# Head pairs side by side in the two halves of the array: two attentions in a two-block kernel

## The chip, the cores and the metric

The kernel runs on one core of a Trainium2 chip, as one program. The metric is the device time of one launch in microseconds; three runs of the kernel before gave 2449.45 to 2453.14, median 2451.6. Engines are named as in the profile: PE is TensorE's matmul, PEld its weight load, DVE is VectorE, ACT is ScalarE, POOL is GpSimd, SP issues the transfers. All engines work through their own instructions in order and meet at semaphores.

## The reference

Two transformer blocks over 512 tokens of width 1024, all in fp32. The first block mixes tokens in two ways side by side and then applies a product-key expert layer (PEER). The second block has two causal attentions side by side. What the change touches is this:

```python
# first block, neighbourhood attention: 8 heads of 64; a query sees a window of 8 x 32 grid keys (masked to 16)
# with a bias, and 256 context keys, in one softmax
s_win = einsum('bcqhd,bkcjhd->bhcqkj', q_r, kb) * scale
s_win = where(col_ok, s_win + bias, -inf)
s_ctx = einsum('bcqhd,blhd->bhcql', q_r, k_ctx) * scale
p = softmax(concatenate([s_win, s_ctx], -1))
o = einsum(p_win, vb) + einsum(p_ctx, v_ctx)
# beside it: a bidirectional gated linear recurrence, 4 heads of 128 (S_t = diag(f_t) S_{t-1} + k_t v_t)

# second block, stick-breaking attention, 8 heads of 64, causal, blocks of 128 queries
z = einsum('bhqd,bhkd->bhqk', qb, k) * scale
suffix = reverse_cumsum(log_sigmoid(-z)) - log_sigmoid(-z)
w = where(strict, exp(log_sigmoid(z) + suffix), 0);  out = w @ v
# second block, latent attention, 8 heads, query and key of 64 + 32, value of 64
sc = (q_nope . k_nope + q_pe . k_pe) * scale
p = softmax(where(causal, sc, -inf));  out = p @ v
```

## The kernel before

Tokens are columns and features are partitions; a matmul takes its stationary operand as 128 partitions by up to 128 columns. fp32 matmuls appear in the trace as two records each, transposes as one. PSUM has 8 banks of 128 x 512.

**Mixing stage** (`phase_mix`, lines 571 to 1012). `items` are 32: head pair hp, query block c of 128, and head s of the pair, in that order, so that items 2m and 2m+1 are the two heads of one pair for one query block. Work goes in 36 slots; slot n holds one item at several stages and, from `fill[n]`, one or two steps of the recurrence (44 steps in four units, of which each has the levels 0 to 9 and a read-out; two context steps ahead, two norms behind). The order in each engine's stream is written out by hand:

- PE (lines 812 to 827): `scores(n)` (two products of 256 columns, contraction 64), the recurrence steps (a level is 8 products of 128 columns), `turn(n-2)` (four transposes), `values(n-3)` (four products whose output has 64 rows).
- DVE (lines 1000 to 1012): the recurrence step (`level`: three products in place, then `copied`, two copies out of PSUM), then `item(n)` (lines 899 to 912: add bias or zero and take the maximum), then `inverse(n-1)`.
- ACT (lines 855 to 893): exponential of n, scaling of n-1, copy of the transposed n-2 out of PSUM (`turned_sb`), and every other slot the attention output of a pair.
- POOL (line 686): one product of each level.

`s_sb`, where `item(n)` writes, has three buffers, so `item(n)` waits until `turn(n-3)` is done (line 904). The scores have two PSUM banks, the transposes and the values one each.

**Second block** (`second_block`, line 1812 on). `items` are 64: first the 32 of the stick-breaking kind, then the 32 of the latent one, in each head by head and then by query block i of 128 (the keys seen, `width`, are 128(i+1)). The slots follow the items. Between them stand the products of the weights ("tiles", `TILES2`, each out of a piece of 128 x 1024 weights that ACT rounds to a high part, line 2049, and DVE turns into a low part, line 2177): 20 tiles (`uqm`, `kn`, `kv`) in the stick half, 20 (`sz` 4, `ga` 8, `bra` 8) in the soft half. A tile is three matmuls for each of its input blocks. `AHEAD` is 3: in slot n PE does `scores(n)`, `turn(n-3)`, `values(n-4)` and then the tiles; DVE does `mask(n)`, `finish(n-1)`, low parts, a store every fourth slot and the evacuations of the slot before; ACT does `exps(n)`, high parts, the copy of the transposed n-3, evacuations. In the stick half the query of an odd head has zeros in its lower 64 rows and that of an even head in its upper 64, so that the products contract over all 128 rows; POOL writes the zeros (lines 1912 to 1916), ACT copies a query tile in two halves (lines 2069 and 2070). The value product of a head computes the 128 columns of its pair, and the store (line 2274) takes the 64 rows that are the head's.

## Time and profile before

| | us |
|---|---|
| Median of 3 runs (lowest, highest) | 2451.6 (2449.45, 2453.14) |
| Profiled execution: own time | 2451.39 |
| its span | 2449.6 |
| PE busy in the span | 2250.8 (92%) |
| DVE busy | 1780.1 (73%) |
| ACT busy | 924.3 (38%) |
| POOL busy | 629.7 (26%) |
| Mixing stage, from and to | 291.9 to 526 |
| Second block's attention, stick half, from and to | 2040 to 2151 |
| soft half, from and to | 2151 to 2294 |

A share of busy time is a mean over stages with different limits. PE is busy nearly all the time in the expert layer between 526 and about 1930 us, which the change doesn't touch. In the stages that it touches, PE and DVE work in turns, so one reads there which engine waits, for what, and what is queued behind the waiting instruction.

### The profile page before, as it was taken

How to read it: one execution, taken by the hardware profiler on the slowest of the kernel's cores; microseconds unless marked ns; L12 is line 12 of the kernel's file. 1: busy time of each engine (PE TensorE's matmuls, PEld its weight loads, DVE VectorE, ACT ScalarE, POOL GpSimd, SP SyncE). 2: the span in 40 equal slices, each digit the busy share in tenths (PEclk: the TensorE clock that was granted, in tenths of full speed). 3: DMA queues.
4: the chain of work that ended last, by engine and by line, in shares of the span. 5: the costliest groups of instructions: out<-in, count | busy, mean ns of one | idle time of the engine just before them, and what ended most of it. 6: DMA issues, size and time to landing. Idle time of an engine off the chain costs nothing. (4 is left out here: it accounts for less than half of the span.)

```text
span 2449.6 us, 32335 instructions
## 1 busy us (share of the span) xinstructions
PE 2250.8 (92%) x12803; PEld 2017.8 (82%) x12803; DVE 1780.1 (73%) x2985; ACT 924.3 (38%) x1210; POOL 629.7 (26%) x357
## 2 busy tenths in 40 slices
PE   5999887978998999999999899999999897889997
PEld 3888676756898999899999899999999676677775
DVE  7555687763689999999995687788786657754543
ACT  4222233333232333455553233333333534566332
POOL 0000232311346776533224433333331000000000
PEclk8999998989999999999999999999999999999999
DMA  6567400011236777688889999999996222111221
GB/s 250 206 239 243 146 8 1 1 69 52 94 111 224 238 243 250 248 309 342 322 332 367 361 350 354 361 348 353 359 351 215 79 78 86 44 52 61 78 86 69
DMA packets 178103, 488.73 MB, mean 200 GB/s; under 512 B 13696, under 2 KB 80384, under 8 KB 166432
## 3 DMA queue, kind: packets, MB, share of 16 engines
q1 hardware_dynamic: 141088, 352.43, 41.6%
q0 software_dynamic: 36864, 134.23, 14.2%
q8 instruction: 102, 1.67, 0.3%
q14 instruction: 49, 0.40, 0.1%
HBM read 432.08 MB, written 52.43 MB: 198 GB/s over the span
## 5 line engine op out<-in xcount | busy, mean ns | idle before, releaser
L1066 PE MATMUL ps<-h_high,u_high 128*128 128x384 f32 (+1 forms) x1216 | 430.8, 354 | 43.4 <-POOL u_low L1256 19.1
L1067 PE MATMUL ps<-h_low,u_high 128*128 128x384 f32 (+1 forms) x1216 | 421.4, 347 | 0.0
L1068 PE MATMUL ps<-h_high,u_low 128*128 128x384 f32 (+1 forms) x1216 | 421.2, 346 | 0.0
L1066 PE MATMUL ps<-w_high,v_high 128*128 128x384 f32 x1024 | 344.5, 336 | 10.0 <-DVE w_low L1636 10.0
L1067 PE MATMUL ps<-w_low,v_high 128*128 128x384 f32 x1024 | 343.5, 335 | 0.0
L1068 PE MATMUL ps<-w_high,v_low 128*128 128x384 f32 x1024 | 343.4, 335 | 0.0
L1066 PEld LDWEIGHTS ps<-h_high,u_high 128*128 128x128 f32 x1216 | 231.0, 190 | 58.7 <-POOL u_low L1256 22.1
L1393 ACT ACTIVATE v_high<-v_raw 128x2048 fp32r<-128x2048 f32 x64 | 122.6, 1916 | 346.8 <-PE ps L1068 346.8
L1066 PE MATMUL ps<-h_high,w_high 128*128 128x512 f32 x560 | 227.7, 407 | 25.6 <-DVE h_low L2289 10.3
L1067 PEld LDWEIGHTS ps<-h_low,u_high 128*128 128x128 f32 x1216 | 231.4, 190 | 8.3 <-issue 1.2
L1068 PEld LDWEIGHTS ps<-h_high,u_low 128*128 128x128 f32 x1216 | 231.0, 190 | 8.0
L1067 PE MATMUL ps<-h_low,w_high 128*128 128x512 f32 x560 | 221.8, 396 | 0.0
L1068 PE MATMUL ps<-h_high,w_low 128*128 128x512 f32 x560 | 221.2, 395 | 0.0
L1624 DVE TENSOR_TENSOR v_low<-v_raw,v_high 128x2048 fp32r<-128x2048 f32 x64 | 146.7, 2293 | 101.8 <-ACT v_high L1393 101.8
L1247 POOL DMA_INDIRECT mixT<-in_peer_v,row_index x102 | 147.5, 1446 | 252.3 <-DVE row_sum L1668 235.9
L1066 PEld LDWEIGHTS ps<-w_high,v_high 128*128 128x128 f32 x1024 | 193.4, 189 | 10.6 <-DVE v_low L1624 7.4
L1247 POOL DMA_INDIRECT mixT<-in_peer_u,row_index x103 | 137.9, 1339 | 249.4 <-DVE row_dot L1592 220.8
L1067 PEld LDWEIGHTS ps<-w_low,v_high 128*128 128x128 f32 x1024 | 193.6, 189 | 0.0
L1068 PEld LDWEIGHTS ps<-w_high,v_low 128*128 128x128 f32 x1024 | 193.4, 189 | 0.0
L1459 ACT ACTIVATE gelu<-ps 128x384 f32<-128x384 f32 x128 | 63.7, 500 | 303.4 <-PE ps L1068 161.9
L2177 DVE TENSOR_TENSOR w_low<-w_raw,w_high 128x1024 fp32r<-128x1024 f32 x69 | 84.6, 1226 | 124.7 <-ACT w_high L2049 124.6
L1066 PEld LDWEIGHTS ps<-h_high,w_high 128*128 128x128 f32 x560 | 107.1, 191 | 57.1 <-issue 14.6
(428 smaller groups left out, 4436.8 us busy)
## 6 DMA issues: line engine op xcount, KB each, us to landing
v_raw<-in_peer_v SPq DMA_DIRECT2D x64, 1024.0 KB, 6.8
w_raw<-in_w SPq DMA_DIRECT2D x99, 512.0 KB, 3.7
u_first<-in_uT SPq DMA_DIRECT2D x32, 1024.0 KB, 6.5
u_second<-in_uT SPq DMA_DIRECT2D x32, 1024.0 KB, 6.7
xT<-in_late_w SPq DMA_DIRECT2D x56, 512.0 KB, 4.4
gelu_up<-gelu SPq DMA_DIRECT2D x128, 192.0 KB, 7.2
gates<-gates_sb SPq DMA_DIRECT2D x12, 2048.0 KB, 12.9
weighted<-gelu_up SPq DMA_DIRECT2D x64, 384.0 KB, 6.9
```

The source lines that it names most:

```text
L1066: pe.matmul(out, wh, mh, start=start, stop=False)
L1067: pe.matmul(out, wh, ml, start=False, stop=False)
L1068: return pe.matmul(out, wl, mh, start=False, stop=stop)
L1247: pool.indirect_dma_start(out=row_of(total), out_offset=None, in_=table, in_offset=bass.IndirectOffsetOnAxis(ap=row_no[:, n:n + 1], axis=0))\
L1393: act.activation(v_high[:, g % 2], v_raw[:, g % 2], ACT.Copy).then_inc(v_hi, 1)
L1459: act.activation(gel[:, x % 4, :], ps[:, x % 4, 0:DENSE], ACT.Gelu).then_inc(u_ev, 1)
L1624: dve.tensor_tensor(v_low[:, g % 2], v_raw[:, g % 2], v_high[:, g % 2].bitcast(F32), ALU.subtract)\
L2177: dve.tensor_tensor(wlo[:, i % SPLITS, :], raw[:, i % RAWS, :], whi[:, i % SPLITS, :].bitcast(F32), ALU.subtract).then_inc(w_low, 1)
```

## The change

Both attentions go by head pairs.

In the mixing stage, PE computes the scores of items n and n+1 together in even slots, first the window product of one head on rows 0 to 63 and of the other on rows 64 to 127, then the same for the context keys. The value products of both heads of the pair n-4 are done in even slots too, block by block in turns, one in the left and one in the right 64 columns, and now ahead of the transposes. DVE takes the item of an odd slot ahead of its recurrence steps, that of an even slot behind them as before, and waits for the scores of the pair. The number of buffers stays.

In the second block the items of a pair stand side by side in the list, and a slot is a pair (34 slots for 69). PE: `scores(p)`, tiles, `values(p-2)`, two transposes of p-1. DVE: two masks, low parts with the evacuations of the same slot, a store, two finishes. ACT: two `exps`, high parts with evacuations, two copies. The stick-breaking scores contract over 64 rows, the heads of a pair in the two halves; the zeros, the waits for them and the second query buffers go. The value products are 64 columns wide, two side by side; a store takes a whole pair, so there are 8 instead of 16. The `ga` tiles come ahead of the `sz` tiles, and the soft half takes them from its first slot on.

The diff, with its small renamings (`AHEAD + 1` to 4, the `scored` wait of `mask` as in `item`) left out:

```diff
@@ -688,17 +688,18 @@
         def _(pe):
-            def scores(i):
-                h, c = items[i]
-                a, hp = DH * (h % 2), h // 2
+            def scores_of_pair(i):
+                hp, c = items[i][0] // 2, items[i][1]
                 if i >= 2:
-                    pe.wait_ge(maxed, 2 * (i - 1))
-                q = k.qT[a:a + DH, hp, c * P:(c + 1) * P]
+                    pe.wait_ge(maxed, 2 * i)
                 k0 = min(max(QB * c - KB // 4, 0), GW - KB)
-                win = k.kT[a:a + DH, hp, 0:T].rearrange("p (r x) -> p r x", r=ROWS)[:, :, k0:k0 + KB]
-                pe.matmul(ps[:, i % 2, 0:WIN], q, win, start=True, stop=True)
-                pe.matmul(ps[:, i % 2, WIN:512], q, k.kT[a:a + DH, hp, T:T + C], start=True, stop=True)\
-                  .then_inc(scored, 1)
+                rows = [slice(0, DH), slice(DH, P)]
+                for s, a in enumerate(rows):
+                    win = k.kT[a, hp, 0:T].rearrange("p (r x) -> p r x", r=ROWS)[:, :, k0:k0 + KB]
+                    pe.matmul(ps[:, s, 0:WIN], k.qT[a, hp, c * P:(c + 1) * P], win, start=True, stop=True)
+                for s, a in enumerate(rows):
+                    pe.matmul(ps[:, s, WIN:512], k.qT[a, hp, c * P:(c + 1) * P], k.kT[a, hp, T:T + C], start=True,
+                              stop=True).then_inc(scored, 1)
@@ -708,18 +709,19 @@
-            def values(i):
-                h, c = items[i]
-                pair = i // 2
-                pe.wait_ge(turned_sb, i + 1)
-                if i % 2 == 0 and pair:
-                    pe.wait_ge(stored, pair)
-                a = DH * (h % 2)
+            def values_of_pair(i):
+                first_head, c = items[i]
+                pe.wait_ge(turned_sb, i + 2)
+                if i:
+                    pe.wait_ge(stored, i // 2)
                 for j in range(4):
-                    v = (k.vw[:, 2 * c + j, :] if j < 2 else k.vc[:, j - 2, :])[:, h * DH:(h + 1) * DH]
-                    last = pe.matmul(ps[a:a + DH, 3, 0:P], v, pT[:, i % 2, j * P:(j + 1) * P],
-                                     start=j == 0, stop=j == 3)
-                last.then_inc(summed, 1)
+                    v = k.vw[:, 2 * c + j, :] if j < 2 else k.vc[:, j - 2, :]
+                    for s in range(2):
+                        h = first_head + s
+                        last = pe.matmul(ps[DH * s:DH * (s + 1), 3, 0:P], v[:, h * DH:(h + 1) * DH],
+                                         pT[:, s, j * P:(j + 1) * P], start=j == 0, stop=j == 3)
+                        if j == 3:
+                            last.then_inc(summed, 1)
@@ -810,8 +812,8 @@
             for n in range(SLOTS_N):
-                if n < N:
-                    scores(n)
+                if n < N and n % 2 == 0:
+                    scores_of_pair(n)
                 for kind, x, s in fill[n]:
@@ -821,10 +823,10 @@
                         norms(x)
+                if 0 <= n - 4 < N and n % 2 == 0:
+                    values_of_pair(n - 4)
                 if 0 <= n - 2 < N:
                     turn(n - 2)
-                if 0 <= n - 3 < N:
-                    values(n - 3)
...
@@ -880,7 +882,7 @@
                     if i >= 2:
-                        act.wait_ge(summed, i - 1)
+                        act.wait_ge(summed, 2 * (i // 2))
                     if i == 0:
...
@@ -899,7 +901,7 @@
                 dve.wait_ge(table, variant[c] + 1)
-                dve.wait_ge(scored, n + 1)
+                dve.wait_ge(scored, 2 * (n // 2) + 2)
                 if n >= 3:
...
@@ -998,12 +1000,14 @@
             for n in range(SLOTS_N):
+                if n < N and n % 2:
+                    item(n)
                 for kind, x, s in fill[n]:
                         read_out(x)
-                if n < N:
+                if n < N and n % 2 == 0:
                     item(n)
...
@@ -1726,10 +1730,10 @@
     piece("kv", 0, [("kv", t) for t in range(4)])
+    for i in range(8):
+        piece("ga", i, [("ga", i)])
     for i in range(4):
         piece("sz", i, [("sz", i)])
-    for i in range(8):
-        piece("ga", i, [("ga", i)])
     for i in range(4):
...
@@ -1815,8 +1818,9 @@
     TT = T // P
-    items = [(kind, h, i) for kind in ("stick", "soft") for h in range(NH) for i in range(TT)]
+    items = [(kind, 2 * hp + s, i) for kind in ("stick", "soft") for hp in range(NH // 2) for i in range(TT) for s in range(2)]
     N = len(items)
+    PAIRS, HALF = N // 2, N // 4
     TB = (6, 7)
...
@@ -1880,13 +1881,13 @@
-        early, late = list(range(PROJECTED, tile_no("sz", 0))), list(range(tile_no("sz", 0), ATTENDED))
-        slots = N + AHEAD + 2
-        fill = {n: [] for n in range(slots)}
+        early, late = list(range(PROJECTED, tile_no("ga", 0))), list(range(tile_no("ga", 0), ATTENDED))
+        slots = PAIRS + 2
+        fill = {p: [] for p in range(slots)}
         for x, j in enumerate(early):
-            fill[1 + x * 31 // len(early)].append(j)
+            fill[x * HALF // len(early)].append(j)
         for x, j in enumerate(late):
-            fill[N // 2 + 4 + x * (N // 2 - 4 + AHEAD) // len(late)].append(j)
+            fill[HALF + x * (slots - HALF) // len(late)].append(j)
...
@@ -1908,12 +1909,6 @@
             pool.memset(prod[:, T - 1:T], 1.0).then_inc(made, 1)
-            pool.wait_ge(made, 3)
-            pool.memset(sq[DH:P], 0.0).then_inc(zeroed, 1)
-            for hp, odd in enumerate(q_odd):
-                pool.wait_ge(zeroed, hp + 1)
-                pool.memset(odd[0:DH], 0.0).then_inc(zeroed, 1)
-            pool.wait_ge(zeroed, 5)
             pool.wait_ge(made, 3)
...
@@ -1975,43 +1970,46 @@
-            def scores(n):
-                kind, h, i = items[n]
-                if n >= 2:
-                    pe.wait_ge(acted, n - 1)
-                if n == 0:
+            def scores(p):
+                kind, h, i = items[2 * p]
+                if p:
+                    pe.wait_ge(acted, 2 * p)
+                if p == 0:
                     pe.wait_ge(act_read, read_by(BY_ACT, PROJECTED))
-                if n == N // 2:
-                    pe.wait_ge(act_read, read_by(BY_ACT, tile_no("sz", 0)))
-                    pe.wait_ge(dve_read, read_by(BY_DVE, tile_no("sz", 0)))
+                if p == HALF:
+                    pe.wait_ge(act_read, read_by(BY_ACT, tile_no("ga", 0)))
+                    pe.wait_ge(dve_read, read_by(BY_DVE, tile_no("ga", 0)))
                     pe.wait_ge(mk_rot, 1)
-                if n == 0:
-                    pe.wait_ge(zeroed, 5)
-                if kind == "stick":
-                    q, key = q_odd[h // 2] if h % 2 else sq[:, h // 2], sk[:, h // 2]
-                else:
-                    q, key = mq[0:QKD, h], mk[0:QKD, h]
-                pe.matmul(ps[:, n % 2, 0:width(n)], q[:, i * P:(i + 1) * P], key[:, 0:width(n)], start=True,
-                          stop=True).then_inc(scored, 1)
+                for s in range(2):
+                    if kind == "stick":
+                        a = slice(DH * s, DH * (s + 1))
+                        q, key = sq[a, h // 2], sk[a, h // 2]
+                    else:
+                        q, key = mq[0:QKD, h + s], mk[0:QKD, h + s]
+                    pe.matmul(ps[:, s, 0:width(2 * p)], q[:, i * P:(i + 1) * P], key[:, 0:width(2 * p)], start=True,
+                              stop=True).then_inc(scored, 1)
                 for j in range(items[n][2] + 1):
-                    last = pe.transpose(ps[:, 2 + n % 2, j * P:(j + 1) * P], w[:, n % (AHEAD + 1), j * P:(j + 1) * P], k.ident[:])
+                    last = pe.transpose(ps[:, 2 + n % 2, j * P:(j + 1) * P], w[:, n % 4, j * P:(j + 1) * P], k.ident[:])
                 last.then_inc(turned, 1)
-            def values(n):
-                kind, h, i = items[n]
-                v, head = (sv if kind == "stick" else mv), n // TT
-                pe.wait_ge(turned_sb, n + 1)
-                if n % TT == 0 and head >= 2:
-                    pe.wait_ge(stored, head - 1)
+            def values(p):
+                kind, h, i = items[2 * p]
+                v, heads = (sv if kind == "stick" else mv), p // TT
+                pe.wait_ge(turned_sb, 2 * p + 2)
+                if i == 0 and heads >= 2:
+                    pe.wait_ge(stored, heads - 1)
                 for j in range(i + 1):
-                    last = pe.matmul(ps[:, 4 + head % 2, i * P:(i + 1) * P], v[:, j, h // 2 * P:(h // 2 + 1) * P],
-                                     pT[:, n % 2, j * P:(j + 1) * P], start=j == 0, stop=j == i)
-                last.then_inc(summed, 1)
+                    for s in range(2):
+                        last = pe.matmul(ps[DH * s:DH * (s + 1), 4 + heads % 2, i * P:(i + 1) * P],
+                                         v[:, j, (h + s) * DH:(h + s + 1) * DH], pT[:, s, j * P:(j + 1) * P],
+                                         start=j == 0, stop=j == i)
+                        if j == i:
+                            last.then_inc(summed, 1)
@@ -2020,15 +2018,16 @@
                     last.then_inc(n_sum, 1)
-            for n in range(slots):
-                if n < N:
-                    scores(n)
-                if 0 <= n - AHEAD < N:
-                    turn(n - AHEAD)
-                if 0 <= n - AHEAD - 1 < N:
-                    values(n - AHEAD - 1)
-                for j in fill[n]:
+            for p in range(slots):
+                if p < PAIRS:
+                    scores(p)
+                for j in fill[p]:
                     tile(j)
+                if p >= 2:
+                    values(p - 2)
+                if 1 <= p <= PAIRS:
+                    turn(2 * p - 2)
+                    turn(2 * p - 1)
             for j in range(ATTENDED, len(TILES2)):
...
                 if n >= 2:
-                    act.wait_ge(summed, n - 1)
+                    act.wait_ge(summed, 2 * (n // 2))
                 act.activation(pT[:, n % 2, 0:width(n)], ps[:, 2 + n % 2, 0:width(n)], ACT.Copy).then_inc(turned_sb, 1)
...
@@ -2138,18 +2135,17 @@
                         act.activation(ghi[:, t, :], M[:, t, :], ACT.Copy).then_inc(t_high, 1)
-            for n in range(slots):
-                if n < N:
-                    exps(n)
-                for j in fill[n]:
+            for p in range(slots):
+                if p < PAIRS:
+                    exps(2 * p)
+                    exps(2 * p + 1)
+                for j in fill[p]:
                     if j in FIRST2:
                         high(TILES2[j][2] + 1)
-                if 0 <= n - AHEAD < N:
-                    turned_out(n - AHEAD)
-                for j in fill[n - 1] if n else []:
                     evac(j)
-            for j in fill[slots - 1]:
-                evac(j)
+                if 1 <= p <= PAIRS:
+                    turned_out(2 * p - 2)
+                    turned_out(2 * p - 1)
             for j in range(ATTENDED, len(TILES2)):
...
-            def store(head):
-                dve.wait_ge(summed, TT * head + TT)
-                if head == 0:
+            def store(heads):
+                dve.wait_ge(summed, 2 * TT * (heads + 1))
+                if heads == 0:
                     dve.wait_ge(mk_rot, 1)
-                rows = slice(DH * (head % 2), DH * (head % 2) + DH)
-                o = (so if head < NH else mo)[rows, head // 2 % 4, :]
-                dve.tensor_copy(o, ps[rows, 4 + head % 2, :]).then_inc(stored, 1)
+                o = (so if heads < NH // 2 else mo)[:, heads % (NH // 2), :]
+                dve.tensor_copy(o, ps[:, 4 + heads % 2, :]).then_inc(stored, 1)
@@ -2325,20 +2320,19 @@
             dve.wait_ge(made, 3)
-            for n in range(slots):
-                if n < N:
-                    mask(n)
-                if 0 <= n - 1 < N:
-                    finish(n - 1)
-                for j in fill[n]:
+            for p in range(slots):
+                if p < PAIRS:
+                    mask(2 * p)
+                    mask(2 * p + 1)
+                for j in fill[p]:
                     if j in FIRST2:
                         low(TILES2[j][2] + 1)
-                if n >= TT + AHEAD + 1 and (n - AHEAD - 1) % TT == 0:
-                    store((n - AHEAD - 1) // TT - 1)
-                for j in fill[n - 1] if n else []:
                     evac(j)
-            for j in fill[slots - 1]:
-                evac(j)
+                if p >= 2 and (p - 2) % TT == TT - 1:
+                    store((p - 2) // TT)
+                if p < PAIRS:
+                    finish(2 * p)
...
```

## Rows read from the trace of the kernel before

**Rows 1.** Busy time by stretch: start:end, length, us of each engine, PEclk.

```profile
291.90:526.00 234.10, 198.24 (x1288) 162.18 (x1288) 170.16 (x380) 84.50 (x168) 76.27 (x42) 0.96 0.04 14
...
2040.00:2151.00 111.00, 89.36 (x460) 68.81 (x461) 87.63 (x156) 59.77 (x139) 0.00 (x0) 0.96 0.16 53
2151.00:2294.00 143.00, 133.82 (x680) 108.16 (x679) 76.98 (x187) 85.12 (x146) 0.00 (x0) 1.00 0.18 60
```

**Rows 2.** Timeline of mixing, DVE: start, us, engine, line, op, count [idle before].

```profile
362.75 0.41 DVE L905 CUSTOM_DVE_ANT_1 s_sb<-ps,bias 128x256 f32<-128x256 f32 x1
...
363.69 0.67 DVE L961 TENSOR_TENSOR qd<-hq,fx 128x512 f32<-128x512 f32 x1
...
365.72 1.35 DVE L930 COPY_PREDICATED A_diag<-pred,ps 128x512 f32<-128x512 uint8 x2
...
367.06 0.42 DVE L905 CUSTOM_DVE_ANT_1 s_sb<-ps,bias 128x256 f32<-128x256 f32 x1
```

**Rows 3.** The same timeline, PE.

```profile
358.50 0.70 PE L699 MATMUL ps<-kT,qT 64*128 64x256 f32 x2
...
365.80 0.70 PE L699 MATMUL ps<-kT,qT 64*128 64x256 f32 x2
...
366.86 2.05 PE L759 MATMUL ps<-qd,kd 128*128 128x128 f32 x16
...
368.74 0.60 PE L708 MATMUL ps<-ident,s_sb 128*128 128x128 f32 x4
...
369.27 0.65 PE L720 MATMUL ps<-w_raw,vw 128*64 128x128 f32 x4
...
370.29 0.70 PE L699 MATMUL ps<-kT,qT 64*128 64x256 f32 x2
```

**Rows 4.** Waits in mixing: who <- for whom: us in total, times, longest.

```profile
DVE s_sb L905 <- PE ps L700: 34.4, 4, 11.4
```

**Rows 5.** Timeline of PE in mixing, after gaps.

```profile
297.02 2.05 PE L735 MATMUL ps<-ic,qd 128*128 128x128 f32 x16 [2.98 <-ACT qd L869]
...
459.12 3.63 PE L776 MATMUL ps<-qd,kd 128*128 128x256 f32 x8 [3.26 <-ACT w_raw L838]
...
508.79 1.97 PE L776 MATMUL ps<-qd,kd 128*128 128x256 f32 x8 [2.21 <-ACT w_raw L838]
```

**Rows 6.** Timeline of PE in mixing, a read-out with full-height products.

```profile
348.53 1.03 PE L801 MATMUL ps<-w_raw,ix 128*128 128x256 f32 x4
349.39 1.02 PE L793 MATMUL ps<-qd,ctx_state 128*128 128x512 f32 x2
```

**Rows 7.** Groups, 2040 to 2296: line, engine, op | busy us, mean ns | idle.

```profile
L2177 DVE TENSOR_TENSOR w_low<-w_raw,w_high 128x1024 fp32r<-128x1024 f32 x28 | 34.3, 1225 | 33.8 <-ACT w_high L2049 33.8
L2259 DVE TENSOR_TENSOR_SCAN at_prod<-at_rest,zeros 128x127 f32<-128x127 f32 (+3 forms) x32 | 26.1, 816 | 1.0 <-ACT at_rest L2101 0.5 <-issue 0.2
L2262 DVE TENSOR_TENSOR at_w<-at_w,at_prod 128x128 f32<-128x128 f32 (+3 forms) x32 | 15.8, 492 | 1.1
...
L2188 DVE TENSOR_TENSOR soft_out<-ps,cosT 32x512 f32<-32x512 f32 x8 | 5.5, 689 | 0.2
...
L2049 ACT ACTIVATE w_high<-w_raw 128x1024 fp32r<-128x1024 f32 x28 | 29.5, 1054 | 0.0
...
L2100 ACT ACTIVATE at_w<-ps 128x128 f32<-128x128 f32 (+3 forms) x32 | 14.1, 440 | 46.5 <-DVE ps L2245 46.5
```

**Rows 8.** Soft half: the gate chain, a tile on PE (timeline), and PE's waits.

```profile
2160.96 1.28 ACT L2087
...
2165.07 0.69 DVE g_low L2203
...
2219.35 0.48 PE L1066 MATMUL ps<-h_high,w_high 128*128 128x512 f32 x1
...
2224.89 0.59 PE L1994 MATMUL ps<-mqkv 96*128 96x256 f32 x2
...
PE ps L2012 <- ACT at_wT L2110: 8.6, 11, 1.4
```

More of the change, by code:

```diff
@@ L1747 @@
 TILES2, PIECES2, PROJECTED, ATTENDED = second_tiles()
-AHEAD = 3
 BY_ACT = {"cq", "ckv", "sq", "sk", "uqm", "kn", "kv", "sz", "ga", "mz", "gb"}
@@ L1830, in second_block @@
         ghi, glo = sb("g2_high", [P, 5, T], F32R), sb("g2_low", [P, 5, T], F32R)
-        w = sb("at_w", [P, AHEAD + 1, T])
+        w = sb("at_w", [P, 4, T])
         rest = sb("at_rest", [P, 2, T])
@@ L2094, in exps @@
                 act.wait_ge(masked, n + 1)
-                if n > AHEAD:
-                    act.wait_ge(turned, n - AHEAD)
+                if n >= 4:
+                    act.wait_ge(turned, n - 3)
                 if kind == "stick":
@@ L2241, in mask @@
                 W = width(n)
-                dve.wait_ge(scored, n + 1)
+                dve.wait_ge(scored, 2 * (n // 2) + 2)
                 diag = ps[:, n % 2, W - P:W]
@@ L2260, in finish @@
                                                 initial=1.0, op0=ALU.mult, op1=ALU.add))
-                    own = w[:, n % (AHEAD + 1), 0:W]
+                    own = w[:, n % 4, 0:W]
                     dve.tensor_tensor(own, own, prod[:, T - W:T], ALU.mult).then_inc(ready, 1)
@@ L2327, in _ @@
             dve.wait_ge(made, 3)
-            for n in range(slots):
-                if n < N:
-                    mask(n)
-                if 0 <= n - 1 < N:
-                    finish(n - 1)
-                for j in fill[n]:
+            for p in range(slots):
[3 more added lines that the diff above has]
+                for j in fill[p]:
                     if j in FIRST2:
                         low(TILES2[j][2] + 1)
-                if n >= TT + AHEAD + 1 and (n - AHEAD - 1) % TT == 0:
-                    store((n - AHEAD - 1) // TT - 1)
-                for j in fill[n - 1] if n else []:
                     evac(j)
-            for j in fill[slots - 1]:
-                evac(j)
+                if p >= 2 and (p - 2) % TT == TT - 1:
+                    store((p - 2) // TT)
+                if p < PAIRS:
+                    finish(2 * p)
+                    finish(2 * p + 1)
             for j in range(ATTENDED, len(TILES2)):
```

13 lines of the change are left out of this document (4 added, 9 removed).

## The prediction

> **What bounds the kernel now.** I read the busy shares by stretch first, since the diff touches only the mixing stage and the second block's attention. Outside them nothing changes but a few short operations. In the mixing stretch (234 us), VectorE is busy 170 us and PE 198 us; in the two halves of the second attention (111 and 143 us) PE is busy 89 and 134 us [rows 1]. Then the timelines, for how the engines interlock.
>
> In mixing, a slot is one attention item beside one or two steps ("levels") of the recurrence. VectorE: an item with its reciprocal takes 363.69 - 362.75 = 0.94 us, a level 367.06 - 363.69 = 3.37 (three products, 2.03, then two copies of 0.67, 1.34 together, that wait for the level before on PE). Nothing is idle between these [rows 2]. PE, same slot: scores 1.06, level 1.88, transposes 0.53, value product 1.02, together 4.49 us from scores to scores, without a gap [rows 3]. So a slot with one level takes 4.49 us (PE just above VectorE's 4.31), one with two 365.80 - 358.50 = 7.3 (VectorE's turn: 4.31 + 3.3). Both engines are full at once, and each level on PE needs VectorE's copies of the same level: the reader should see a loop with no slack on either side. VectorE's idle time is nearly all in four waits for scores, 34.4 us [rows 4], where a read-out ends a unit.
>
> **Mixing: the new wait.** VectorE has three buffers for the scores it reads (s_sb, item n uses n mod 3), so item n waits until item n-3 has been transposed (`turned`). PE transposes n-3 in slot n-1, after that slot's level. Before, VectorE did the level of slot n first and the item last, so the transposes had a whole level (3.37) to get done. The change puts the item of each odd slot ahead of its level. VectorE then reaches item n (odd) right after item n-1, while PE still has the level of slot n-1 to do, now two items' value products ahead of the transposes too. Behind the waiting item stand VectorE's level, its copies, PE's next level, POOL's product and ScalarE's exponential.
>
> I time it from the end of VectorE's copies in the even slot. PE's level may start 0.1 after the first of the two copies, so at -0.67 + 0.1, and ends 1.88 later, at 1.31. Then two value products V, transposes 0.53 + 0.13 to land (0.7 with the semaphore), then VectorE's item 0.87, three products 2.03, first copy 0.67, and PE's odd level 0.1 + 1.88. Then transposes 0.53, pair scores S, and PE's next even level 1.88.
>
> V and S are not in the trace. Upper ends, no two matmuls side by side: V = 2 x 1.02 = 2.04, S = 2 x 1.06 = 2.12 [rows 3]. Lower ends: a 128-column full-height fp32 record takes 1.88/16 = 0.118 us, and each fp32 product is two records on the same half of the array; the order is two records in one half, two in the other, so a record can pair only with its neighbour over the change of half: 16 value records fit in 9 times, 8 score records in 5. That gives V = 9 x 0.118 = 1.06 and S = 5 x 0.26 = 1.3. The 0.26 is a row of its own kind: 256-column records in half the rows come 1.06/4 = 0.265 us apart [rows 3], full-height ones (349.39 - 348.53)/4 = 0.215 [rows 6]; so half height alone is no gain, only company is. I take the lower ends, since the two halves read other partitions and write other banks or partitions.
>
> The Trainium skill, "TensorE: Matmul & The Clock Gate", Part 3 (Measured speedup vs the span model), gives 3.07 times for four row tiles at once, which speaks for the lower ends; "TensorEngine Tiling (Array Packing)", Key Properties, says that a change of tiling mode drains the engine, which speaks against the change in the second attention. No row here shows two tiles together. The changes of form in rows 3 cost at most some 0.05 us each.
>
> With the lower ends a pair of single-level slots takes 1.31 + 1.06 + 0.7 + 0.87 + 2.03 + 0.67 + 0.1 + 1.88 + 0.53 + 1.3 + 1.88 = 12.33, less the first 1.31, since it is counted from one end of PE's even level to the next: 11.0 us, against 2 x 4.49 = 8.98: +2.0. VectorE alone would need 1.31 + 1.06 + 0.7 + 0.87 + 3.37 + 0.07 + 3.37 = 10.75. With a second level in the even slot VectorE is last, 10.75 + 3.37 = 14.1 against 4.49 + 7.3 = 11.8 (+2.3); in the odd slot PE is, with VectorE's second first copy 3.3 later: 14.4 against 11.8 (+2.6). There are 12 such pairs, four of each kind: +27.6. With the upper ends the same three sums give +3.8, +3.3, +4.4: +46.
>
> Where a unit ends, VectorE already waits for PE (up to 11.4 us [rows 4]); there the odd item waits for transposes instead of scores, which comes out even, but the next unit's first product now stands behind it: +0.9 and +0.7 at two ends, -1 at the norm. At the start item 1 no longer waits for scores behind the context products: -2. Together -1. Mixing: +26 (+45 unpacked).
>
> **The clock.** The new wait leaves PE idle 0.13 + 0.87 + 2.03 + 0.67 + 0.1 = 3.8 us in each pair. After 3.26 us idle, eight records took 3.63 us, after 2.21 us the same eight took 1.97; after 2.98 us sixteen 128-column records still took 2.05 [rows 5], as a level does without a gap [rows 3]. So a gap of 3.8 likely drops PE from its 2.4 to its 1.2 GHz level for about one level: +1.5 us where PE sets the end (four single pairs), about +0.4 in the eight where VectorE's second level covers it: +9. Bounds 0 and 12 x 1.7 = 20.
>
> **Second attention.** Now a slot is a pair. Before, scores of n+1 ran ahead while VectorE finished n-1 and ScalarE did n. Now both score banks belong to one pair, VectorE masks both, waits for ScalarE (activations, then the weight's high part), then does the low part, the evacuation, and only then the two finishes.
> Stick half: a slot with a query tile costs VectorE 0.35, ScalarE four activations at 0.33 to 0.44 and the high part's 0.96 to 1.05 (2.3 taken: they overlap in its pipe), then the low part 1.23, three operations of 0.7 for the evacuation, two finishes at 0.82 + 0.49 = 2.6 [rows 7]: 8.2 us at the narrow widths there; six slots and two double tiles at 3.4 make 56, and the ten others some 4.4 each plus 2.2 for each of four low parts and stores of 0.7 make 55. That is 111 us, as before [rows 1]. PE's own savings here (values, scores 64 high) lie under it. Taken as 0; bounds -10 and +12, since averages hide how widths line up.
> Soft half: PE-bound. A gate tile is 24 matmuls in 2224.89 - 2219.35 = 5.54 us [rows 8], and the 160 value records at 0.118 are 18.9 us and could shrink to 9/16, -8.3; scores stay (96 rows). PE's 8.6 us of waits for the transposed copies [rows 8] go, since values now run two pairs late. In their place: the gated tiles (sz) now come just before the branch tiles, whose first waits for the last low part of the gate; that chain takes 2165.07 + 0.69 - 2160.96 = 4.8 us a tile [rows 8], with the slot's masks and activations ahead of it, and ends some 5.6 us after PE gets there by my count (estimate); the clock adds 1.7. Net -9.6; taken as -6 with 3 for changes of form. Upper end +8 (nothing packs, VectorE's chain decides), lower -17.
> Zero halves of the query: POOL's five memsets and one of two copies a tile go. They lie beside the projection's products; worth 0, at most -2.
>
> **Sum.** +26 + 9 + 0 - 6 = +29, on a profiled execution of 2451.4 us (span 2449.6), which stands at the median of 2451.6: 2480 us. The likeliest case's own range is 2465 to 2495.
>
> **Rivals.**
> Nothing runs side by side: same wait, V and S at upper ends: 45 + 9 - 1 + 3 = +56, 2507. For it: no row of company, and the fp32 pairs stay on one half. Against: the halves share nothing.
> Faster: the odd item finds its transposes done. It decides if PE is ahead by 2.1 us when VectorE ends the even slot, or if that slack is given back at the unit ends, where VectorE stands 34.4 us anyway [rows 4]. Then mixing loses nothing (0 to -6 from PE's shorter slots) and the soft half gives -9 and the stick half -5: 2451 - 17 = 2434. Against: the level on PE can't start before VectorE's copy, so PE can't be ahead.
> The pair grain costs in the stick half: with no finish to do while ScalarE works, each of 13 low parts waits 1.2 us more and isn't paid back: 2480 + 15 = 2495.
> No effect of any of it (both parts cancel): 2451.
>
> **How the numbers follow.** Forecast 0.44, unpacked 0.20, faster 0.20, pair grain 0.12, cancel 0.04. About 0.2% (5 us) is what a measurement of this kernel tells from no change. Slower 0.76, same 0.04, faster 0.20. The range 2446 to 2510 leaves out most of the faster case and the tail of the unpacked.
>
> **What would show it.** Right: the mixing stretch grows from 234 to some 265-270 us; VectorE's item line waits on PE's transposes about 2 us in each of some 12 odd slots; PE idles 3.8 us before each odd level, with a lower granted clock; value records of the two halves start in overlapping pairs. Wrong: no VectorE wait on the transposes in odd slots; a stick half off 111 by over 10 us; a gap before the first branch tile missing; score records spaced 0.26 us (nothing packs).

## The result, and the profile after

The changed kernel takes 2492.5 us (median of 4 runs, 2490.6 to 2494.8) against 2451.0 (4 runs beside it): a ratio of 1.0165, 95% interval 1.0151 to 1.018, some 41 us slower. The forecast was 2480, and the range 2446 to 2510. The execution read here has a span of 2488.8 us (2449.6 before).

To set the traces side by side I use the start of the first product of three stages: the expert layer, the second block's attention, and its soft half.

| stretch | before | after | difference |
|---|---|---|---|
| mixing, up to the expert layer's first product | 291.9 to 537.7 | 291.4 to 586.7 | +49 |
| expert layer and projections, up to the first scores | 1502.7 | 1500.8 | -2 |
| stick half, up to the soft half's first scores | 100.9 | 109.0 | +8 |
| soft half, up to the last value product | 152.1 | 136.1 | -16 |

The ends of the first stretch are these rows of PE's timeline (start, us, what ran, idle before and who ended it), first of the kernel before:

```profile
537.73 0.77 PE L1066 MATMUL ps<-h_high,u_high 128*128 128x512 f32 x1 [14.60 <-DVE h_low L1488]
```

and of the changed one:

```profile
586.67 0.77 PE L1070 MATMUL ps<-h_high,u_high 128*128 128x512 f32 x1 [14.59 <-DVE h_low L1492]
```

The busy shares by stretch of the changed kernel (start:end, length, us of PE, PEld, DVE, ACT, POOL, granted clock, DMA share, GB/s) answer to [rows 1]. In mixing, PE's busy time hardly changed (195 us for 198), nor did VectorE's (172 for 170); the granted clock went from 0.96 to 0.84. PE's 195 us isn't the same work: with a fourth score buffer (below) the same products took 167 us there, so slow products fill up what the pairs save:

```profile
291.40:573.00 281.60, 195.25 (x1288) 163.51 (x1288) 171.94 (x380) 87.38 (x168) 74.16 (x42) 0.84 0.04 12
...
2087.40:2196.40 109.00, 80.73 (x412) 50.92 (x413) 78.49 (x132) 53.00 (x125) 0.00 (x0) 0.84 0.16 54
2196.40:2332.50 136.10, 131.25 (x722) 100.09 (x724) 80.62 (x203) 85.36 (x154) 0.00 (x0) 1.00 0.20 63
```

VectorE's timeline in mixing, two slots, answers to [rows 2]. L907 is the first operation of an item. The even item starts at 388.02, the odd one right behind it has to wait for the transposes (L709), and only then come the products of the level (L963):

```profile
388.02 0.42 DVE L907 CUSTOM_DVE_ANT_1 s_sb<-ps,bias 128x256 f32<-128x256 f32 x1 [1.45 <-PE ps L701]
...
391.61 0.42 DVE L907 CUSTOM_DVE_ANT_1 s_sb<-ps,bias 128x256 f32<-128x256 f32 x1 [2.56 <-PE ps L709]
...
392.49 0.68 DVE L963 TENSOR_TENSOR qd<-hq,fx 128x512 f32<-128x512 f32 x1
...
399.20 0.73 DVE L932 COPY_PREDICATED A_diag<-pred,ps 128x512 f32<-128x512 uint8 x1 [0.67 <-PE ps L761]
```

PE's timeline over the same stretch answers to [rows 3]:

```profile
382.05 3.75 PE L761 MATMUL ps<-qd,kd 128*128 128x128 f32 x16 [3.98 <-DVE A_diag L932]
385.59 1.06 PE L709 MATMUL ps<-ident,s_sb 128*128 128x128 f32 x4
386.58 0.82 PE L699 MATMUL ps<-kT,qT 64*128 64x256 f32 x4
387.25 0.59 PE L701 MATMUL ps<-kT,qT 64*128 64x256 f32 x4
387.77 2.05 PE L761 MATMUL ps<-qd,kd 128*128 128x128 f32 x16
389.75 0.66 PE L721 MATMUL ps<-w_raw,vw 128*64 128x128 f32 x8
390.24 0.61 PE L721 MATMUL ps<-w_raw,vc 128*64 128x128 f32 x8
390.78 0.65 PE L709 MATMUL ps<-ident,s_sb 128*128 128x128 f32 x4
395.41 6.25 PE L761 MATMUL ps<-qd,kd 128*128 128x128 f32 x32 [3.98 <-DVE A_diag L932]
401.49 0.60 PE L709 MATMUL ps<-ident,s_sb 128*128 128x128 f32 x4
402.02 0.70 PE L699 MATMUL ps<-kT,qT 64*128 64x256 f32 x4
402.56 0.60 PE L701 MATMUL ps<-kT,qT 64*128 64x256 f32 x4
403.36 2.02 PE L761 MATMUL ps<-qd,kd 128*128 128x128 f32 x16 [0.20 <-DVE A_diag L932]
```

Three things are to be seen. PE idles 3.98 us ahead of the first level of an odd slot, in twelve such slots. The level behind such a gap takes 3.75 us (two in a row 6.25), where the one at 387.77 takes 2.05: the clock is at its 1.2 GHz level for most of it. Of the twelve, the full levels alone in their slot take 2.64 to 3.75 us, at granted clocks of 0.73 to 0.50. And the heads do run side by side: the two groups of four score records start 402.56 - 402.02 = 0.54 us apart, so the eight take 1.08, where four took 1.06 before [rows 3], and sixteen value records take 390.78 - 389.75 = 1.03, where eight took 1.02.

The waits in mixing (who <- for whom: us in total, times, longest), beside [rows 4]:

```profile
DVE s_sb L907 <- PE ps L709: 57.1, 15, 10.6
...
PE ps L761 <- DVE A_diag L932: 42.7, 14, 4.0
...
DVE s_sb L907 <- PE ps L701: 7.7, 6, 1.8
```

**Where the 49 us of mixing are.** The starts of the even items on VectorE give the length of each pair of slots. Eleven pairs with levels stand whole between two items of one unit; in the traces of before and after they take, in order:

```
before   8.53 11.81  8.09  8.81 11.82  8.09  8.80 11.81 10.15  8.56 11.81
after   12.36 15.72 11.65 13.23 15.71 11.55 12.81 15.02 13.41 12.33 15.73
more     3.83  3.91  3.56  4.42  3.89  3.46  4.01  3.21  3.26  3.77  3.92
```

That is 41.2 us, 3.75 a pair. The four stretches that hold a start or an end of a unit give +0.0, +1.2, -1.3 and +2.0, and the tail behind the last item, with the twelfth pair in it, +6.2. With the first item 0.5 earlier this is +49.

How well one trace tells this is seen where the same mixing code was traced more than once. In three runs with the changed code the eleven pairs take 147.4, 149.5 and 151.8 us and the expert layer's first product starts at 585.9 to 591.7; in two runs with the old code they take 108.3 and 109.4, and it starts at 537.7 and 542.7. So the +41 is good to some 2 us, the +49 to some 5, and a stretch's +1 or +2 says nothing by itself.

### The profile page after: what moved, and what is told of

It is laid out like the page before. It is cut to its first block and busy times, and to the rows that moved or that the text cites. A ratio compares the mean times of both kernels' runs of the same rounds, so it can differ in the third digit from the quotient of the medians.

```text
span 2488.8 us, 32296 instructions
## 1 busy us (share of the span) xinstructions
PE 2236.9 (90%) x12803; PEld 1991.7 (80%) x12803; DVE 1779.1 (71%) x2977; ACT 919.7 (37%) x1202; POOL 624.8 (25%) x352
```

## The experiments

Each was timed beside the kernel before, whose median there lay between 2451.8 and 2452.5. Edits are given against the changed kernel.

**Either part alone.** First the mixing stage of after with the second block of before, then the reverse.

> The mixing stage as changed, the second block as before. Theory (the changed mixing loses about 49 us, the second block wins about 8): 2499 us, 1.020 of before, and the stretch up to the first product of the expert layer ends at 587 us of the span, not 538. Rival (the loss comes from how the stages share transfers or clock): 2485 or less, since part of the loss would need the second block's change too.

Measured: 2501.7 us, 1.0202 (1.0188 to 1.0216). The first expert product starts at 591.7.

> The second block as changed, the mixing stage as before. Theory: the gain of the second attention stands alone: 2442 to 2444 us (0.9965 of before), stick half 8 us longer, soft half 16 us shorter. Rival (the gain was a side effect of the later start or of the clock after the slower mixing): 2451, no change.

Measured: 2444.8 us, 0.9967 (0.9954 to 0.9979). Stick half 109.3 us, soft half 136.1. So the loss is all in mixing, and the second block gains some 8 us. The two parts hardly touch each other: +49 and -8 give the +41 of the whole.

**Four score buffers.** The odd item still goes first, but waits for the item four back:

```diff
-        s_sb = sb("s_sb", [P, 3, 512])
+        s_sb = sb("s_sb", [P, 4, 512])
...
-                if n >= 3:
-                    dve.wait_ge(turned, n - 2)
+                if n >= 4:
+                    dve.wait_ge(turned, n - 3)
```

> All of the change, with a fourth buffer for the scores in the mixing stage, so that the item of an odd slot waits for transposes of the slot before. Theory of the prediction (that wait, and the clock that falls in the gap it makes, is the loss): the waits of VectorE on the transposes go (57 us to under 10), the gap of 3.98 us before each odd level goes, mixing is back at 246 us or a little under, 2437 to 2443 us. Rival (the loss is in the pair grain of the scores or in PE's changes of tiling form): 2480 or more.

Measured: 2434.0 us, 0.9929 (0.9915 to 0.9944), first expert product at 531.3. This is 58 us less than the changed kernel, and less than the kernel before. In PE's timeline there, of an even slot's end and the odd slot behind it, the gap ahead of the odd slot's first level is 1.35 us, and both of its levels come at the full clock. Only three levels of the whole stage are mostly at the lower clock (at 309.86, 319.61 and 455.24), two at the stage's start and one at the end of a unit.

```profile
371.95 0.66 PE L721 MATMUL ps<-w_raw,vw 128*64 128x128 f32 x8
372.43 0.61 PE L721 MATMUL ps<-w_raw,vc 128*64 128x128 f32 x8
372.97 0.65 PE L709 MATMUL ps<-ident,s_sb 128*128 128x128 f32 x4
374.98 2.02 PE L761 MATMUL ps<-qd,kd 128*128 128x128 f32 x16 [1.35 <-DVE A_diag L932]
378.25 2.02 PE L761 MATMUL ps<-qd,kd 128*128 128x128 f32 x16 [1.25 <-DVE A_diag L932]
```

The steady pairs are back at their length of before (8.46 for 8.81, 11.74 for 11.82): there VectorE's own work is the limit, and PE's shorter slots buy next to nothing. The gain of 6 us is at the ends of the units (17.3 for 19.9 us and 18.5 for 20.6), where PE alone has work.

**Levels ahead of odd items.** Three buffers again, the packed products kept, and VectorE in the order of before:

```diff
-                if n < N and n % 2:
-                    item(n)
...
-                if n < N and n % 2 == 0:
+                if n < N:
                     item(n)
```

> All of the change but VectorE's order: in odd slots too, the recurrence step comes ahead of the item, three buffers as before. Theory: the order alone made the wait; with the level between, the transposes are done in time, PE's pair scores wait for the odd item for about 1 us in the shadow of VectorE's three products, and VectorE is busy without a gap: 8.62 us a pair of single-level slots, 2436 to 2443 us. Rival (item first was needed so that PE's next pair of scores isn't late): PE waits for the odd item 1 to 2 us a pair on the path, mixing about 20 us over before, 2460 or more.

Measured: 2441.9 us, 0.9954 (0.994 to 0.9968), first expert product at 538.7. This takes the wait away from the other side, and 51 of the 58 us go with it. VectorE's waits for L709 are 30.7 us in three places, all at ends of units; the kernel before stood 29.4 us for scores in the same three.

**The gap filled.** To tell the wait from the clock, PE gets three products of 512 columns, of no use, in the gap at the end of the even slot (bank 0, written over by the next scores), and waits ahead of them until the even item has been read out of the bank:

```diff
+                if n % 2 == 0 and 2 <= n < N and any(f[0] == "level" for f in fill[n + 1]):
+                    pe.wait_ge(maxed, 2 * n + 2)
+                    for _ in range(3):
+                        pe.matmul(ps[:, 0, :], k.ident[:], k.zeros[:], start=True, stop=True)
```

> All of the change; in even slots PE does three more 512-column fp32 products (2.6 us, into a score bank that is free by then, result not used) after its transposes, where it otherwise waits 3.98 us for VectorE. Theory of the prediction: the gap lowers PE's clock, and the slow stretch behind it costs 9 us; with the gap filled the odd levels take 2.05 us instead of 3.4 to 3.75 and the time falls to 2478 to 2486. Rival (the slow stretch lies in VectorE's shadow, or the clock falls anyway): 2490 to 2494.

Measured: 2476.5 us, 1.0102 (1.0085 to 1.0119), first expert product at 570.4. More work on PE, and 16 us less than the changed kernel:

```profile
375.64 0.66 PE L709 MATMUL ps<-ident,s_sb 128*128 128x128 f32 x4
376.14 2.74 PE L833 MATMUL ps<-zeros,ident 128*128 128x512 f32 x6
380.27 2.02 PE L761 MATMUL ps<-qd,kd 128*128 128x128 f32 x16 [1.40 <-DVE A_diag L936]
```

The level behind the filler takes 2.02 us, not 3.75, and so do all full levels behind the twelve fillers inside units. VectorE's waits for the transposes stay (58.9 us for 57.1). The same eleven pairs are here 26.6 us longer than before, 2.42 each: this is the wait without the clock. The other 14.6 us of the 41.2, 1.33 a pair, are the clock's.

**Heads in turn.** Does the company of the two heads need records that alternate? In mixing, both products of one head go ahead of those of the other:

```diff
-                for s, a in enumerate(rows):
...
-                for j in range(4):
-                    for s in range(2):
+                for s in range(2):
+                    for j in range(4):
```

> All of the change, but in the mixing stage the products of one head are all issued ahead of those of the other, so that neighbours in PE's order lie in the same half. Theory: the company of the two halves is real and worth 1.06 us for the scores and 1.03 for the values of each pair; without it 16 pairs lose 1.5 to 2.1 us each: 2516 to 2526. Rival (records of one half are as quick, the trace only draws them together): 2490 to 2495.

Measured: 2500.2 us, 1.0196 (1.0182 to 1.0209), first expert product at 595.6. That is 8 us more than with alternating records, and well below what I expected. PE's timeline shows why:

```profile
408.42 0.71 PE L699 MATMUL ps<-kT,qT 64*128 64x256 f32 x4
408.95 0.60 PE L700 MATMUL ps<-kT,qT 64*128 64x256 f32 x4
409.81 2.02 PE L760 MATMUL ps<-qd,kd 128*128 128x128 f32 x16 [0.26 <-DVE A_diag L931]
411.76 0.65 PE L720 MATMUL ps<-w_raw,vw 128*64 128x128 f32 x4
412.25 0.27 PE L720 MATMUL ps<-w_raw,vc 128*64 128x128 f32 x1
412.26 0.32 PE L720 MATMUL ps<-w_raw,vw 128*64 128x128 f32 x1
412.36 0.27 PE L720 MATMUL ps<-w_raw,vc 128*64 128x128 f32 x1
412.42 0.27 PE L720 MATMUL ps<-w_raw,vw 128*64 128x128 f32 x1
...
412.75 0.60 PE L720 MATMUL ps<-w_raw,vc 128*64 128x128 f32 x4
413.28 0.66 PE L708 MATMUL ps<-ident,s_sb 128*128 128x128 f32 x4
```

The program has vw, vc of the left head, then vw, vc of the right one. In the trace the right head's vw records run among the left head's vc records, one every 0.055 us or so: records of a free half start ahead of earlier ones that wait for theirs. Only the first four and the last four are alone, so sixteen take 1.52 us, neither 1.03 nor 2.04. The eight score records still take 2 x 0.53 = 1.06. The experiment thus took away only half of the value products' company, and does not show what a fully unpacked change would cost; that stays untried, since each head's data lie in one half.

In the second attention the value products alone were put in turn in the same way:

> All of the change, but in the second attention the value products of one head are issued ahead of those of the other. Theory (soft half bound by PE, company worth half of 18.9 us there, little in the stick half): 2500 to 2503. Rival (soft half's gain came from the waits that went with the later values): 2492 to 2495.

Measured: 2495.0 us, 1.0183 (1.0168 to 1.0198): 2.5 us more, which the times can only just tell from nothing, and which is the end of the rival's range. The stages tell more: sixteen records take 1.51 us for 1.02, and the soft half takes 140.6 us, against 136.1 in the changed kernel and 136.1 to 136.2 in the five other traces that have its second block unaltered. So side by side does pay in the soft half, 4.4 us for the part of it that this order takes away, and the rival as it was put (all of the gain came from the waits) fails.

**The stick half.** Two tries at its +8, both with four score buffers, to be held against 2434.0 and a half of 109.0. First VectorE's finishes of pair p-1 go right behind the masks of pair p, ahead of the low parts:

```diff
+                if 1 <= p <= PAIRS:
+                    finish(2 * p - 2)
+                    finish(2 * p - 1)
...
-                if p < PAIRS:
-                    finish(2 * p)
-                    finish(2 * p + 1)
```

> Four score buffers in mixing (as the run that gave 2434), and in the second attention VectorE finishes pair p-1 right after the masks of pair p, ahead of the low parts, so that it has work while ScalarE does its activations. Theory (the stick half lost 8 us because VectorE has nothing to do between masks and low part): low parts wait less, stick half 5 to 10 us shorter, 2425 to 2430. Rival (the activations of the next pair need the finishes for their buffer, so the wait only moves to ScalarE): 2434 to 2445.

Measured: 2436.3 us, 0.9933 (0.992 to 0.9947); the half takes 112.6. The rival came true. ScalarE's activations of the next pair now stand for the finishes (L2258), and the wait for the high parts only falls from 19.4 to 16.7 us:

```profile
ACT at_w L2097 <- DVE at_w L2258: 49.9, 30, 5.0
...
DVE w_low L2173 <- ACT w_high L2048: 16.7, 9, 2.2
```

So this order moves the wait. It doesn't tell what the half would take if the low parts waited less.

Then filler on PE in that half, to hold its clock up:

> The version with four score buffers, and in the stick half one product of zeros over 512 columns (about 0.9 us of PE, nothing reads it) behind the value products of each of 15 slots. In that half the changed kernel's PE runs at a granted clock of 0.84 on average against 0.96 before, and some 35 tile products and four groups of scores came at the lower level; put together these are some 10 us longer than their like. If the clock is what makes the stick half 109 us instead of 101: the granted clock there goes up to 0.93 or more and the half comes down to 101 to 105 us, the kernel to some 2429 (from 2434.0). If the grain of the pairs sets it (VectorE's two finishes wait one after the other, and PE waits for them whatever its clock): the clock goes up all the same, the half stays at 108 to 111, and the kernel at 2433 to 2437. If the filler itself delays the transposes on PE: half above 112, kernel 2438 or more.

```diff
+                if 2 <= p <= HALF:
+                    pe.matmul(ps[:, 2, :], k.ident[:], k.zeros[:], start=True, stop=True)
```

Measured: 2441.6 us, 0.995 (0.9932 to 0.9968), the half 111.5. Of its shares by stretch, first with four buffers, then with the filler as well, each over the half as it lies in its own trace (the second row reaches 1 us beyond it), the granted clock is the third number from the end:

```profile
2030.30:2139.30 109.00, 80.81 (x413) 50.97 (x413) 78.51 (x132) 53.01 (x125) 0.00 (x0) 0.84 0.17 54
```

```profile
2035.40:2148.00 112.60, 91.01 (x447) 56.04 (x448) 79.51 (x133) 54.69 (x127) 0.00 (x0) 0.89 0.16 52
```

The clock came up less than halfway, short of the 0.93 that was expected of it, and the half got 2.5 us longer, with 13.5 us of filler in it. VectorE's wait for the high parts is the same 19.4 us. So no gain from the clock is seen, but what the lower clock costs in this half isn't shown: the filler may take back what the clock gives. That the order of VectorE's and ScalarE's work in a pair makes the half long is argued from the waits below. (The two traces are 10 us apart; 3 of it lie in mixing, whose code is the same, 2 between, and 2.5 in the soft half. Only the half's own length is read here.)

**The gate tiles.** Four buffers, and `sz` ahead of `ga` as before the change:

> The version with four score buffers, but the sz tiles ahead of the ga tiles again, as before the change. My prediction put a stall of 5.6 us ahead of the first branch tile on the new order; the trace of the changed kernel has 1.0 us there. If the order costs nothing beside that: the stall goes, 2433 to 2434 against 2434.0 with the new order, within what can be measured. If the new order is part of why the soft half came down by 16 us (the branch tiles wait for gates that the old order leaves to the end): the soft half grows by 3 us or more from 136, kernel 2437 or more. If the stall is larger in the paired form without it being seen as one wait: 2431 or less.

Measured: 2433.7 us, 0.9925 (0.9909 to 0.994), against 2434.0; the soft half takes 135.3 us for 136.1. The new order of the tiles is no part of the gain; at most it costs the 0.8.

The version to keep is the change with a fourth score buffer, 0.7% faster than the kernel before.

## Why the prediction came out right, and where its sizes were off

**The new wait.** It is where it was put, and it is the cause: VectorE stands for the transposes in 15 slots, 57.1 us in all. Three of them, 28.5 us, are at ends of units, where it stood 29.4 us for scores before; the new wait is the other twelve, 28.6 us or 2.4 each, 2.56 in the one shown (2.2 by the prediction's terms: 1.31 + 1.06 + 0.7 - 0.87). Two independent edits that take it away, one in the buffers and one in the order, bring back 58 and 51 us. The pair lengths of the prediction gave +2.0, +2.3 and +2.6, or 2.3 in the mean. With the clock held up the runs show 2.42, between 2.15 and 2.77. Some 1 us of each wait is the value products, which the change also moved ahead of the transposes; no run puts these two back in the old order with three buffers, a small edit that stays untried.

**Company of the heads.** V = 1.06 and S = 1.3 were taken, with 2.04 and 2.12 as upper ends. The trace has 1.03 and 1.08. The picture behind the numbers, that a record can pair only with its neighbour, was wrong, as the heads in turn show; it happened to give nearly the same V. The rival that nothing runs side by side (2507) fell. The rule cited on the drain at a change of tiling mode (the Trainium skill, "TensorEngine Tiling (Array Packing)", Key Properties) can't be ruled out by these rows, but no gap of that kind over some 0.1 us shows in them. The one cited for the lower ends (the same skill, "TensorE: Matmul & The Clock Gate", Part 3, Measured speedup vs the span model) is for four row tiles; for the two halves here the trace agrees in kind: two products in 1.01 to 1.02 times the time of one.

**The clock, mis-sized.** The gap is 3.98 us (3.8 forecast), and the level behind it is 3.75 - 2.02 = 1.73 longer. I charged it in full in four pairs and at 0.4 in the eight where VectorE's second level should cover it: 9 us. The filler shows 14.6 in the eleven pairs and 16 in all: 1.7 a pair where the even slot has the second level, 1.2 where the odd one has, and 1.1 in single pairs. There was no cover: in the timeline of VectorE above it then waits 1.45 us for scores behind the slow level (388.02) and 0.67 for the second copy (399.20), in just such pairs. A slow level is itself a link of the loop between the engines, whichever of them was the longer. The error was to treat an engine's slack in the mean as cover for one late product. The bound of 20 was sound.

**Unit ends, not told.** Forecast -1, of which -2 at the start. Item 1's wait for scores (4.9 us before) did go, but the first item of the second pair starts only 0.5 us earlier; the other ends within mixing add 2.0, and the tail 2.5 beside its pair. So mixing is 12 x 2.42 = 29, clock 16, and starts and ends 4, against 27.6, 9 and -1. The 4 is no more than what two traces of one code differ by in mixing (5 us), so its sign isn't shown. What each of these ends waits for I haven't taken apart; VectorE's two longest waits for the transposes, 10.6 us the longer, lie there.

**The stick half, 8 instead of 0.** The step that failed is the base of the comparison. The prediction adds up 16 slots and gets 111 us; from the half's first scores to those of the soft half the changed kernel took 109.0. But it set this beside the 111 us of [rows 1], which run to the last value product of the half's kind (2151), some ten us into the soft half; from scores to scores the kernel before took 100.9. With like bounds the prediction's own sum says +10.

What makes the half longer is argued and not shown. A rival (+15, chance 0.12) had said it: with no finish to do while ScalarE works, VectorE waits for each high part. In the stick half that wait went from the first of these rows to the second, 12.4 us more, and PE waits where it hardly did, up to 6.0 us for a low part, and for both of ScalarE's activations before the next pair's scores:

```profile
DVE w_low L2177 <- ACT w_high L2049: 7.0, 9, 1.0
```

```profile
DVE w_low L2173 <- ACT w_high L2048: 19.4, 9, 2.9
PEld ps L1070 <- DVE w_low L2173: 15.4, 7, 6.0
PEld ps L1989 <- ACT at_rest L2098: 12.8, 9, 2.1
```

PE is idle 28.3 us in the half, where it was 19.0, and its busy time hardly fell (80.7 us for 81.9), though the products of two heads run side by side: more of them come at the lower clock (granted 0.84 on average for 0.97). The finishes put earlier only moved the wait, and the filler raised the clock too little, so how the 8 us divide between waits and clock, and which order would bring them back, stays open.

**The soft half, -16 instead of -6.** Groups of PE there (busy us, mean ns | idle before), before:

```profile
L2012 PE MATMUL ps<-at_wT,mqkv 128*128 128x128 f32 x160 | 24.6, 285 | 8.6 <-ACT at_wT L2110 8.6
L1994 PE MATMUL ps<-mqkv 96*128 96x128 f32 (+3 forms) x64 | 22.8, 438 | 1.2 <-ACT at_rest L2101 1.2
```

and after:

```profile
L1989 PE MATMUL ps<-mqkv 96*128 96x128 f32 (+3 forms) x64 | 20.2, 437 | 2.2 <-ACT at_rest L2098 1.2 <-ACT at_w L2100 1.0
L1070 PE MATMUL ps<-g_high,w_high 128*128 128x512 f32 x32 | 14.2, 442 | 1.0 <-DVE g_low L2199 1.0
...
L2008 PE MATMUL ps<-at_wT,mqkv 128*64 128x128 f32 x160 | 12.3, 283 | 0.0
```

The busy time of a group holds the ends of its records, which lie over the start of the next group, so the 12.3 us between the two rows of value products is more than PE saved. Counted from each record's start to that of the next, the value products took 18.1 us before and 11.2 after, 6.9 less (8.3 forecast), and the scores 17.6 and 14.2, 3.4 less, where I had charged 3 for changes of form. In all, PE is busy 9.5 us less in the half (131.6 for 141.0) and idle 6.6 us less (4.8 for 11.4).

The waits for the transposed copies are gone, as forecast. The mis-sized term is the stall ahead of the first branch tile: 1.0 us, not 5.6, since my count had put all of the slot's masks and activations ahead of the last gate's chain. The 1.7 for the clock didn't come either (granted clock 1.00 in the row above), nor the 3 for changes of form. With these three at 1.0, 0 and 0 the prediction's other terms give -8.3 - 8.6 + 1.0 = -15.9. The lower bound of -17 held.

**The sum.** Forecast 26 + 9 + 0 - 6 = +29; measured 33 + 16 + 8 - 16, and -2 in the stages between, = +39 in the spans (+41 in the medians). The errors in mixing and the stick half (+22) and in the soft half and between (-12) are of opposite sign, so the 2480 is nearer than its terms deserve. The -2 between is within what traces of one code differ by there. By its number alone the rival of the pair grain (2495) is nearer to the 2492.5, but it gets there with 15 in the stick half, which gave 8, and without the clock's other 7. The faster rival (2434) named the condition rightly: with four buffers the odd item finds its transposes done, and the kernel took 2434.0. That its number fits so well is luck: it took at most -6 for mixing, -9 for the soft half and -5 for the stick half, and the trace of that run has -6.5, -16 and +8, with -4 between.

## What to carry to other kernels

When two engines are both full in a loop, moving one step earlier in one engine's order can make its buffer the new wait: count, for each buffer, how much work of the other engine lies between the release and the next use, and price a further buffer before giving up the change. A gap that this opens on PE is paid twice if the granted clock falls in it, and here slack of the other engine didn't cover the slower products. Products that share the array paid where PE was the limit (the soft half, the ends of units), and brought next to nothing where it wasn't. And when a sum of slots is set beside a stretch of the old trace, both must begin and end at the same event.

## What the runs showed of the hardware

- Products in the two halves of the array overlap fully, by rows and by columns: eight 256-column records of half the rows in 1.08 us, and sixteen 128-column ones of half the columns in 1.03, about twice the rate of [rows 3].
- Records needn't alternate in the program: the other half's run ahead of earlier ones that wait (16 in 1.52 us, 0.055 apart in the middle). The Trainium skill, "TensorE: Matmul & The Clock Gate", Part 3 (The mechanism), says that products start and end strictly in program order; this trace doesn't agree for products in different halves, at least not for the starts, as ends are modelled.
- After 3.98 us without work a single 16-record level took 2.64 to 3.75 us; with 2.74 us of filler in that gap, 2.02 each time. Thirteen fillers saved 16 us while they added work.
- The length of the last gap alone doesn't tell the level of the clock: in the changed kernel a level after 2.95 us of idle took 2.05 us, and with four buffers one after 2.62 us took 3.62.
